# One sum unit per pass in two output projections, and an earlier output bias, in an RG-LRU and latent-attention decoder kernel

## The chip, the cores and the metric

The kernel runs on one core of a Trainium2 chip. The metric is the device time of one launch in microseconds; each kernel's time is the median of its runs.

## What is computed (the reference, cut)

A trunk of two layers over 256 positions of width 2048, all in float32: an RG-LRU block, a SwiGLU feed-forward network, an attention block with a compressed key and value, and a second feed-forward network.

```
h = x
h = h + rglru_block(rmsnorm(h))     # ... (gelu(gate_br) * rec) @ w_out + b_out
h = h + swiglu(rmsnorm(h))          # D_FF = 5632
k, v = shared_kv(rmsnorm(h))
h = h + mla_block(rmsnorm(h), k, v) # ... o.reshape(256, 2048) @ w_o
h = h + swiglu(rmsnorm(h))
```

The change concerns the two square products of 2048 by 2048, `... @ w_out + b_out` and `... @ w_o`. They are called projections here, with d = 0 (LRU) and d = 2 (attention); the down products of the feed-forward networks are d = 1 and d = 3.

## The kernel before

**Splitting.** Each float32 operand is split in a high part (a copy in the type float32r, made by ScalarE) and a low part (the operand minus the high part, made by VectorE). A product of two tiles is three matmuls: high times high, high times low, low times high. The weights come in chunks of 1 MB: SyncE's queue loads chunk c in a slot of `raw`, ScalarE's `split` writes `w_hi`, VectorE's `split` (L1129) writes the low part and raises `w_lo_done`, and TensorE computes one unit per chunk and raises `chunk_used`.

**Units.** In the projections and the feed-forward networks a chunk is 2 tiles of depth (k) by 2 of width (n), and with the 2 tiles of positions a unit is 8 products, 24 matmuls of 128x512 (`plain_unit`). A sum unit (`sum_unit`) computes the same 8 products as 7 by Winograd's scheme, 21 matmuls. For it VectorE makes four sums of 128x128 of the activations (the sides) and three sums of 128x512 of the weights (`sums`), ScalarE and VectorE split them too, and three of the products of all sum units of a pass gather in the second half of the PSUM banks (`shared`), out of which ScalarE (`p1_out`) and VectorE (`shared_add`, `shared_to_h`) read them and add them to h. Before the change only the feed-forward networks have sum units.

**Projections.** `project(d)` is two passes of 8 units, one for each half of the width; unit n has chunk DOWN_C[d] + n. Half 0 gathers in banks 0 to 3, half 1 in banks 4 to 7. ScalarE and VectorE are in the loop `for n in range(12)`, where iteration n splits chunk n + 4. At units 13 and 14 TensorE also transposes the finished first blocks of h, which the next stage wants. `stationary` splits a group of four tiles of the activations.

**Slots.** There are five slots. A chunk of a feed-forward network has its low part in place (`raw_lo` is `raw`), so its slot is free for the next load at `chunk_used`. The chunks of the other stages have their low parts in `w_lo`, so the slot is free at `w_lo_done`, earlier. The LRU stages use four slots, the attention and its projection four others in the order of `MID_SLOTS`.

**Around them.** The stages are, in order: the recurrent half of the LRU's input product (first block from the start, chunks 0 to 15), the gates (4 chunks), the gelu half (16 chunks, called gelu chunks 0 to 15), projection 0, up and down of the network, the attention, projection 2, up and down. The order on every engine is that of the program, written by hand; nothing is reordered. In the gelu stage ScalarE also makes exponentials, squares, tanh and square roots for the scan, and VectorE's `gain_of_input` (L1587, L1590) and the scans stand between the splits. GpSimd adds the output bias to h (L1827): two instructions of 128x2048, after a load of 1 MB of its own, behind a wait on `y_done` 4, the end of the gelu stage. GpSimd also makes half of the low part of two chunks per block of the network (L1850).

Of the kernel before, what the change touches and what calls it, by code (L numbers as in the profile page):

```python
# [18 lines left out]
F32 = mybir.dt.float32  # L19
# [6 lines left out]
P = 128  # L26
# [119 lines left out]
def build_program(nc, a, out):  # L146
    x, positions = a["x"], a["positions"]
    ctx = ExitStack()
    with ctx:
# [24 lines left out]
        raw_lo_t = sb("raw_lo", [P, SLOTS, KC, W], F32R)  # L174
        w_hi_t = sb("w_hi", [P, SLOTS, KC, W], F32R)
# [238 lines left out]
        def _(sp_):  # L414
# [5 lines left out]
            def load(c, src, dst=None):  # L420
# [7 lines left out]
                else:  # L428
                    sp_.wait_ge(chunk_used if in_ffn(before) else w_lo_done, before + 1)
# [225 lines left out]
        def _(act):  # L655
# [74 lines left out]
            def split_sums(c, q, e, tiles=UP_TILES, g_no=None):  # L730
# [19 lines left out]
            def down_split(f, n):  # L750

                c = DOWN_C[2 * f + 1] + n
                if down_sum(n):
                    g_no = down_sum_no(n)
                    split_sums(c, down_unit_no(f, n), g_no % 2, DOWN_TILES, 2 * len(DOWN_SUMS) * f + g_no)
                else:
                    split(c)

            def two_pass(f):
                d = 2 * f + 1  # L760
                c0 = DOWN_C[d]

                def p1_out(n, half):

                    act.wait_ge(chunk_used, c0 + n + 1)
                    act.wait_ge(h_shared, 2 * f + half)
                    A.activation(gtmp[:, 0, :], banks_of(half == 0)[1][0][:, :], ACT.Copy).then_inc(p1_done, 1)

                for n in range(DOWN_UNITS - 4):
# [3 lines left out]
                    if v == DOWN_SUMS[-1]:  # L773
                        p1_out(n, half)
# [27 lines left out]
            def project(d):  # L802
                for n in range(KT - 4):
                    if d == 0 and n == 5:
                        rope_sines()
                    if n in (1, 3) or n == d == 0:
                        g = (n + 3) // 2
# [4 lines left out]
                    split(DOWN_C[d] + n + 4)  # L812
# [309 lines left out]
        def _(dve):  # L1122
# [94 lines left out]

            def down_sums(f, n):

                d, g_no = 2 * f + 1, down_sum_no(n)  # L1220
                v, o, j = n % PASS_UNITS, 2 * len(DOWN_SUMS) * f + g_no, g_no % 3
                dve.wait_ge(gT_act, FB * f + v // 2 + 1)
                slot_free(dve, DOWN_C[d] + n)
                a11, a21 = feat[:, 2 * v, 0:P], feat[:, 2 * v, P:SEQ]
                a12, a22 = feat[:, 2 * v + 1, 0:P], feat[:, 2 * v + 1, P:SEQ]
                V.tensor_tensor(s_raw[:, j, 0, :], a22, a21, ALU.subtract).then_inc(g_sum_step, 1)
                V.tensor_tensor(s_raw[:, j, 2, :], a11, a21, ALU.subtract)
                dve.wait_ge(g_sum_step, 2 * o + 1)
                V.scalar_tensor_tensor(out=s_raw[:, j, 1, :], in0=s_raw[:, j, 0, :], scalar=-1.0, in1=a11,
                                       op0=ALU.mult, op1=ALU.subtract).then_inc(g_sum_step, 1)  # L1230
                dve.wait_ge(g_sum_step, 2 * o + 2)
                V.tensor_tensor(s_raw[:, j, 3, :], a12, s_raw[:, j, 1, :], ALU.add).then_inc(g_sum, 1)
                sums(DOWN_C[d] + n, down_unit_no(f, n), g_no % 2, DOWN_TILES)

            def down_split(f, n):

                c = DOWN_C[2 * f + 1] + n
                if down_sum(n):
                    g_no = down_sum_no(n)
                    o, j = 2 * len(DOWN_SUMS) * f + g_no, g_no % 3  # L1240
                    dve.wait_ge(g_sum_hi, o + 1)
                    V.tensor_tensor(s_lo[:, j, :, :], s_raw[:, j, :, :], s_hi[:, j, :, :].bitcast(F32),
                                    ALU.subtract).then_inc(g_sum_lo, 1)
# [6 lines left out]
            def results_to_h(d, half, units):  # L1250

                result = pass_banks(d, half)
                if d % 2:
                    dve.wait_ge(h_shared, d + half)
                elif d == 0 and half == 0:
                    dve.wait_ge(bout_added, 1)
# [29 lines left out]

            def project(d):
                for n in range(KT - 4):
                    if n in (1, 3) or n == d == 0:
                        g = (n + 3) // 2  # L1290
# [3 lines left out]
                    split(DOWN_C[d] + n + 4)  # L1294
                into_next(d, DOWN_C[d] + KT, KT // 2)

            def two_pass(f):
                d = 2 * f + 1

                def shared_to_h(half):  # L1300

                    n = 4 * f + 2 * half
                    shared_add(banks_of(half == 0)[1], SUM_BLOCKS * f + FB + half,
                               (FB + 2) * f + FB + half)
                    for t in range(NT):
                        hb = h[:, t, (2 * half) * W:(2 * half + 1) * W]
# [1041 lines left out]
```

## Time and profile before

| | |
|---|---|
| median of 3 runs | 1965.88 us (1965.7 to 1966.6) |
| the profiled execution | 1965.88 us, of which its span is 1964.1 us |
| granted TensorE clock, mean | 1.00 of 2.4 GHz |
| TensorE busy | 1956.0 us, 100% |
| VectorE, ScalarE, GpSimd busy | 1728.3, 1168.4, 163.3 us |
| DMA | 378.62 MB, mean 193 GB/s |

Busy times are shares of one execution. A busy TensorE is one whose matmuls overlap without a gap; its speed is read from the starts of two matmuls, not from the duration of one.

### The profile page before, as it was taken

The page shows a single profiled execution, that of the slowest core. Times are in us where ns is not written, and L with a number is a line of the kernel's source. Part 1 is how long each engine was busy: PE and PEld are TensorE (multiplying, and loading weights), DVE is VectorE, ACT ScalarE, POOL GpSimd, SP SyncE. Part 2 cuts the span into 40 slices and gives each one's busy share as a digit, 9 for nine tenths or more (in the row PEclk, how much of TensorE's full clock was granted, in tenths as well). Part 3 has the DMA queues.
Part 4 walks back from the last instruction along what each step waited for, and adds up shares of the span by engine and source line. Part 5 has one row for each costly group of instructions (what it writes and reads, how often), then busy time and mean ns, then how long its engine had stood idle before and what let it go on. Part 6 is the DMA issues. An engine that isn't in the chain of part 4 may idle for free.

```text
span 1964.1 us, 23870 instructions
## 1 busy us (share of the span) xinstructions
PE 1956.0 (100%) x9342; PEld 1645.4 (84%) x9342; DVE 1728.3 (88%) x1957; ACT 1168.4 (59%) x1477; POOL 163.3 (8%) x147
## 2 busy tenths in 40 slices
PE   9999999999999999999999999999999999999999
PEld 8898888888888888888898888888888888888887
DVE  8979847999999999999976886489999999999997
ACT  5488546556565556666666664566555565666563
POOL 1000210110001101000002110000001100010000
PEclk9999999999999999999999999999999999999999
DMA  8654663665666656666564335456565666666664
GB/s 283 209 199 164 222 215 129 196 208 196 200 207 196 208 196 198 209 195 205 180 222 148 115 127 194 143 180 210 196 209 198 200 200 201 205 201 201 205 197 148
DMA packets 160685, 378.62 MB, mean 193 GB/s; under 512 B 6298, under 2 KB 11172, under 8 KB 160452
## 3 DMA queue, kind: packets, MB, share of 16 engines
q1 hardware_dynamic: 160276, 376.06, 58.0%
q8 instruction: 69, 1.13, 0.2%
q0 software_dynamic: 272, 1.13, 0.2%
q14 instruction: 36, 0.29, 0.0%
q10 hardware_dynamic: 32, 0.01, 0.0%
HBM read 375.08 MB, written 2.10 MB: 192 GB/s over the span
## 4 chain that ended last, share of the span: by engine, by line
PE 93%; issue 5%; DVE 1%; POOL 1%; ACT 0%; DMA 0%; POOLq 0%; SPq 0%; ACTq 0%
PE bank L1938 78%; PE bank L2134 6%; PE bank L2132 3%; PE bank L1899 2%; PE bank L1931 1%; PE bank L2118 1%; PE bank L1922 1%; DVE w_lo L1129 0%; POOL stats L1880 0%; PE bank L2131 0%; DMA raw<-in_lru_w_in 0%; ACT w_hi L663 0%; POOL stats L1878 0%; PE bank L2098 0%; POOL stats L1876 0%
## 5 line engine op out<-in xcount | busy, mean ns | idle before, releaser
L1938 PE MATMUL bank<-w_hi,act 128*128 128x512 f32 x3416 | 1097.7, 390 | 0.0
L1938 PEld LDWEIGHTS bank<-w_hi,act 128*128 128x128 f32 x3416 | 641.4, 188 | 132.5
L1938 PE MATMUL bank<-raw_lo,act 128*128 128x512 f32 x1452 | 565.2, 389 | 0.0
L663 ACT ACTIVATE w_hi<-raw 128x2048 fp32r<-128x2048 f32 (+2 forms) x238 | 444.3, 1882 | 143.6 <-PE bank L1938 62.8
L1938 PEld LDWEIGHTS bank<-raw_lo,act 128*128 128x128 f32 x1452 | 272.7, 188 | 56.2
L744 ACT ACTIVATE w_lo<-t_raw 128x1024 fp32r<-128x1024 f32 x110 | 116.4, 1058 | 278.6 <-DVE t_raw L1186 278.6
L1129 DVE TENSOR_TENSOR raw_lo<-raw,w_hi 128x2048 fp32r<-128x2048 f32 x110 | 250.3, 2286 | 9.6 <-ACT w_hi L663 9.4
L1199 DVE TENSOR_TENSOR raw_lo<-raw,w_hi 128x2048 fp32r<-128x2048 f32 x110 | 251.1, 2283 | 0.0
L1129 DVE TENSOR_TENSOR w_lo<-raw,w_hi 128x2048 fp32r<-128x2048 f32 (+1 forms) x84 | 183.1, 2190 | 64.4 <-ACT w_hi L663 64.0
L1938 PE MATMUL bank<-w_lo,act 128*128 128x512 f32 x586 | 192.5, 389 | 0.0
L1850 POOL TENSOR_TENSOR raw_lo<-raw,w_hi 128x1024 fp32r<-128x1024 f32 x44 | 106.7, 2425 | 821.1 <-ACT gtmp L849 738.0
L2134 PE MATMUL bank<-act,w_hi 128*128 128x512 f32 x480 | 169.0, 396 | 0.0
L1938 PE MATMUL bank<-w_lo 128*128 128x512 f32 x528 | 148.2, 389 | 0.0
L2132 PE MATMUL bank<-act,w_lo 128*128 128x256 f32 x512 | 142.6, 281 | 0.2 <-DVE act L1150 0.2
L1186 DVE TENSOR_TENSOR t_raw<-raw 128x1024 f32<-128x1024 f32 x110 | 134.1, 1219 | 0.8 <-issue 0.2
L1195 DVE TENSOR_TENSOR w_lo<-t_raw,w_lo 128x1024 fp32r<-128x1024 f32 x110 | 134.1, 1219 | 0.3 <-ACT w_lo L744 0.3
L1938 PEld LDWEIGHTS bank<-w_lo,act 128*128 128x128 f32 x586 | 110.0, 188 | 22.6
L1899 PE MATMUL bank<-w_hi,act 128*128 128x512 f32 (+2 forms) x448 | 124.5, 354 | 0.3 <-DVE act L1150 0.2
L1938 PE MATMUL bank<-w_hi,w_lo 128*128 128x512 f32 x352 | 122.7, 389 | 0.0
L741 ACT ACTIVATE w_hi<-raw 128x1024 fp32r<-128x1024 f32 x110 | 115.5, 1050 | 3.8 <-DMA raw<-in_ffn_w_in 3.2
L1938 PEld LDWEIGHTS bank<-w_lo 128*128 128x128 f32 x528 | 99.1, 188 | 20.6
L2134 PEld LDWEIGHTS bank<-act,w_hi 128*128 128x128 f32 x480 | 90.1, 188 | 21.2
(246 smaller groups left out, 2403.9 us busy)
## 6 DMA issues: line engine op xcount, KB each, us to landing
raw<-in_ffn_w_in SPq DMA_DIRECT2D x176, 1024.0 KB, 5.4
raw<-in_ffn_w_out SPq DMA_DIRECT2D x88, 1024.0 KB, 5.3
raw<-in_lru_w_in SPq DMA_DIRECT2D x28, 1024.0 KB, 5.6
raw<-in_lru_w_out SPq DMA_DIRECT2D x16, 1024.0 KB, 4.9
raw<-in_w_o SPq DMA_DIRECT2D x16, 1024.0 KB, 5.5
raw<-in_w_ukv SPq DMA_DIRECT2D x8, 1024.0 KB, 5.4
raw<-in_w_uq SPq DMA_DIRECT2D x8, 768.0 KB, 4.6
raw<-in_w_dkv SPq DMA_DIRECT2D x8, 576.0 KB, 3.9
```

Source lines behind the costliest of these rows:

```text
L663: A.activation(flat_chunk(w_hi, SLOT[c], size), flat_chunk(raw, SLOT[c], size), ACT.Copy).then_inc(w_hi_done, 1)
L741: A.activation(hi[:, first, :], own[:, first, :], ACT.Copy)
L744: A.activation(sum_hi_tiles(e)[:, 0:2, :], sum_tiles(t_raw, e)[:, 0:2, :], ACT.Copy).then_inc(sum_hi, 1)
L1129: V.tensor_tensor(low_part(c).rearrange("p k n -> p (k n)")[:, 0:size], flat_chunk(raw, SLOT[c], size), flat_chunk(w_hi, SLOT[c], size).bi ...
L1186: V.tensor_tensor(t13, first, second, ALU.add).then_inc(t_sum, 1)
L1195: V.tensor_tensor(sum_tiles(w_lo_t, e)[:, 0:2, :], sum_tiles(t_raw, e)[:, 0:2, :], sum_hi_tiles(e)[:, 0:2, :].bitcast(F32), ALU.subtract)
L1199: V.tensor_tensor(flat_chunk(raw_lo, SLOT[c], KC * W), flat_chunk(raw, SLOT[c], KC * W), flat_chunk(w_hi, SLOT[c], KC * W).bitcast(F32), A ...
L1850: G.tensor_tensor(raw_lo[SLOT[c]][:, own, :], raw[SLOT[c]][:, own, :], w_hi[SLOT[c]][:, own, :].bitcast(F32), ALU.subtract).then_inc(pool_ ...
L1899: i = T.matmul(outs[t], x_part, wp, start=first and n == 0, stop=last and n == 2)
L1938: i = T.matmul(bank[:, :], x_part, w_part, start=first and n == 0, stop=last and n == 2)
L2132: i = T.matmul(lru_bank(idx, q), wl, act_hi[:, k, :], start=False, stop=False)
L2134: i = T.matmul(bank, wh, x_both, start=False, stop=k == KT - 1)
```

## The change

In each pass of the two projections one unit becomes a sum unit: unit 4 of half 0 and unit 11 of half 1. For that:

- the low parts of both projections' chunks are in place, so their slots are free at `chunk_used`. Projection 2 now has five slots (`slot_of`), projection 0 still four;
- ScalarE and VectorE make the sides and sums of chunks 4 and 11 in iterations 0 and 7, and `shared` is read out in iterations 4 and 11;
- `stationary` of group 2 moves from iteration 1 to 0, that of group 3 from 3 to 2;
- TensorE waits at unit 8, and ahead of the transposes of units 13 and 14, until `shared` has been read;
- the bias is loaded in the high part of slot 4 near the start, and added behind a wait on the last product of the gates (`ix_done` 8) and no more on `y_done` 4. `bout_added` is now awaited by `shared_to_h`.

The other hunks are new counts of the same semaphores, and functions taken out of `two_pass` and `down_sums` word for word.

```diff
+PROJ_SUMS = (4, 11)
...
 def slot_of(c):
-    if not in_ffn(c):
-        return c % 4 if c < C_UP0 else MID_SLOTS[c % 4]
-    return (c - C_UP0) % SLOTS if c < C_DKV else (c - C_UP1 + 2) % SLOTS
+    if c < C_UP0:
+        return c % 4
+    if c < C_DKV:
+        return (c - C_UP0) % SLOTS
+    return MID_SLOTS[c % 4] if c < C_WO else (c - C_WO + 2) % SLOTS
...
-                    sp_.wait_ge(chunk_used if in_ffn(before) else w_lo_done, before + 1)
+                    sp_.wait_ge(chunk_used if in_place(before) else w_lo_done, before + 1)
...
             def project(d):        # ScalarE
                 for n in range(KT - 4):
-                    if n in (1, 3) or n == d == 0:
-                        g = (n + 3) // 2
+                    for g in {0: (2,) if d else (1, 2), 2: (3,)}.get(n, ()):
                         stationary(d, g, wo_slot(g) if d else act_slot(g))
...
-                    split(DOWN_C[d] + n + 4)
+                    if n in PROJ_SHARED:
+                        p1_out(d, PROJ_SHARED[n], n // PROJ_UNITS)
+                    after = n + 4
+                    if after in PROJ_SUMS:
+                        split_sums(DOWN_C[d] + after, proj_unit_no(d, after), PROJ_PLACE[after], DOWN_TILES,
+                                   proj_side_no(d, after), PROJ_SET[after])
+                    else:
+                        split(DOWN_C[d] + after)
...
+            def proj_sums(d, n):        # VectorE
+                kt = 2 * proj_rows(d, n)
+                source_ready(dve, d, kt // 4)
+                dve.wait_ge(chunk_used, DOWN_C[d])
+                make_side(proj_side_no(d, n), kt, PROJ_SET[n])
+                sums(DOWN_C[d] + n, proj_unit_no(d, n), PROJ_PLACE[n], DOWN_TILES)
+            def proj_split(d, n):
+                if n not in PROJ_SUMS:
+                    return split(DOWN_C[d] + n)
+                side_low(proj_side_no(d, n), PROJ_SET[n])
+                split_sums(DOWN_C[d] + n, proj_unit_no(d, n), PROJ_PLACE[n])
...
             def project(d):        # VectorE
                 for n in range(KT - 4):
-                    if n in (1, 3) or n == d == 0:
-                        g = (n + 3) // 2
+                    for g in {0: (2,) if d else (1, 2), 2: (3,)}.get(n, ()):
                         stationary(g, wo_slot(g) if d else act_slot(g), DOWN_G0[d] + g + 1)
                     if n == KT // 2 - 1:
                         results_to_h(d, 0, KT // 2)
-                    split(DOWN_C[d] + n + 4)
+                    if n in PROJ_SHARED:
+                        half = n // PROJ_UNITS
+                        if half:
+                            dve.wait_ge(h_sq, NB * d + 2)
+                        shared_to_h(d, half, SUM_BLOCKS * (d // 2) + half)
+                    if n + 4 in PROJ_SUMS:
+                        proj_sums(d, n + 4)
+                    proj_split(d, n + 4)
...
             rstd(SS_X, RS, 2, D, x_rstd)        # GpSimd
-            pool.wait_ge(y_done, 4)
             pool.dma_start(bout[:, :], a["lru_b_out"][0:1, :].broadcast_to([P, D])).then_inc(bout_in, 16)
             pool.wait_ge(bout_in, 16)
+            pool.wait_ge(ix_done, 8)
             for t in range(NT):
                 i = G.tensor_tensor(h[:, t, :], h[:, t, :], bout[:, :], ALU.add)
...
+                if n == PROJ_UNITS:        # TensorE
+                    pe.wait_ge(u_done, SUM_BLOCKS * (d // 2) + 1)
                 pe.wait_ge(w_lo_done, DOWN_C[d] + n + 1)
-                if v == KT // 2 - 1:
+                if n in PROJ_SUMS:
+                    first = n in (PROJ_SUMS[0], PROJ_SUMS[1])
+                    pe.wait_ge(g_sum_lo, proj_side_no(d, n) + 1)
+                    if first and half:
+                        pe.wait_ge(h_done, NB * d + 2)
+                    elif first and d == 0:
+                        pe.wait_ge(act_hi_done, HI0[0])
+                    elif first:
+                        pe.wait_ge(s_max, 2 * PAIRS)
+                        pe.wait_ge(o_done, PAIRS)
+                    i = sum_unit(c, PROJ_PLACE[n], PROJ_SET[n], k0, result, shared_banks(d, half), first,
+                                 n in PROJ_LAST, None, DOWN_TILES)
+                elif v == KT // 2 - 1:
                     i = last_unit(c, k0, result)
```

## Rows read from the trace of the kernel before

**Rows 1.** The page: busy time of TensorE, its share of the span, instructions.
```profile
PE 1956.0 (100%) x9342; PEld 1645.4 (84%) x9342; DVE 1728.3 (88%) x1957; ACT 1168.4 (59%) x1477; POOL 163.3 (8%) x147
```
**Rows 2.** Busy time by stretch: gelu chunks 11 to 15, projection 0, one network block.
```profile
187.10:214.80 27.70, 27.70 (x161) 24.26 (x161) 25.36 (x35) 13.12 (x14) 0.00 (x0) 1.00 0.76 260
214.80:303.60 88.80, 88.80 (x401) 73.72 (x400) 55.01 (x39) 46.43 (x55) 19.70 (x19) 1.00 0.54 191
343.90:385.70 41.80, 41.80 (x190) 34.61 (x189) 39.60 (x39) 24.74 (x30) 4.83 (x2) 1.00 0.61 201
```
**Rows 3.** Timeline of VectorE, start and length in us: one sum unit's preparation.
```profile
834.52 0.29 DVE L1226 TENSOR_TENSOR t_raw<-feat_all 128x128 f32<-128x128 f32 x1
835.46 1.22 DVE L1186 TENSOR_TENSOR t_raw<-raw 128x1024 f32<-128x1024 f32 x1
842.07 0.69 DVE L1202 TENSOR_TENSOR w_lo<-t_raw,w_lo 128x512 fp32r<-128x512 f32 x1
```
**Rows 4.** Timelines of TensorE, ScalarE and VectorE where projection 2 begins.
```profile
1191.78 0.47 PE L1938 MATMUL bank<-w_hi,act 128*128 128x512 f32 x1
1192.55 1.91 ACT L663 ACTIVATE w_hi<-raw 128x2048 fp32r<-128x2048 f32 x1
1194.36 1.05 ACT L719 ACTIVATE act<-feat_all 128x1024 fp32r<-128x1024 f32 x1
1194.50 2.29 DVE L1129 TENSOR_TENSOR w_lo<-raw,w_hi 128x2048 fp32r<-128x2048 f32 x1 [5.96 <-ACT w_hi L663]
1205.76 1.92 ACT L663 ACTIVATE w_hi<-raw 128x2048 fp32r<-128x2048 f32 x1 [3.52 <-PE bank L1938]
```
**Rows 5.** The tile bout; then GpSimd and VectorE where they are both at work.
```profile
L1827 POOL TENSOR_TENSOR h<-h,bout x2: 6360/6510/6659, 228.3 to 234.7; 128x2048 f32<-128x2048 f32 x2
233.35 3.49 DVE L1129 TENSOR_TENSOR w_lo<-raw,w_hi 128x2048 fp32r<-128x2048 f32 x1 [3.15 <-ACT w_hi L663]
236.76 5.64 DVE L1171 TENSOR_TENSOR act<-feat_all,act 128x1024 fp32r<-128x1024 f32 x1
343.89 2.42 POOL L1850 TENSOR_TENSOR raw_lo<-raw,w_hi 128x1024 fp32r<-128x1024 f32 x1 [35.99 <-ACT gtmp L849]
343.78 0.69 DVE L1210 TENSOR_TENSOR utmp<-gtmp,bank 128x512 f32<-128x512 f32 x1 [2.43 <-ACT gtmp L849]
```
**Rows 6.** Timelines of VectorE, ScalarE and TensorE from the gates to gelu chunk 11.
```profile
126.69 0.69 DVE L1579 TENSOR_TENSOR feat_all<-feat_all,utmp 128x512 f32<-128x512 f32 x1 [0.56 <-ACT utmp L938]
128.49 2.29 DVE L1129 TENSOR_TENSOR w_lo<-raw,w_hi 128x2048 fp32r<-128x2048 f32 x1 [1.11 <-ACT w_hi L663]
138.46 1.23 DVE L1587 SCALAR_TENSOR_TENSOR feat_all<-feat_all 128x1024 f32<-128x1024 f32 x1 [3.42 <-ACT feat_all L960]
141.86 1.06 ACT L958 ACTIVATE feat_all<-feat_all 128x1024 f32<-128x1024 f32 x1
184.61 2.27 DVE L1129 TENSOR_TENSOR w_lo<-raw,w_hi 128x2048 fp32r<-128x2048 f32 x1
187.05 0.28 PE L2132 MATMUL bank<-act,w_lo 128*128 128x256 f32 x1
```
**Rows 7.** The start: one stretch of 10 us, VectorE's split of chunk 7, ScalarE behind chunk 7's unit.
```profile
20.00:30.00 10.00, 10.00 (x62) 8.75 (x60) 8.81 (x16) 7.46 (x13) 1.81 (x2) 1.00 1.05 341
46.11 2.29 DVE L1129 TENSOR_TENSOR w_lo<-raw,w_hi 128x2048 fp32r<-128x2048 f32 x1
56.15 1.21 ACT L923 ACTIVATE utmp<-bank 128x256 f32<-128x256 f32 x4 [3.57 <-PE bank L2134]
```
**Rows 8.** DMA issues (count, size, median us to landing); ScalarE and VectorE at projection 0's end.
```profile
raw<-in_ffn_w_in SPq DMA_DIRECT2D x176, 1024.0 KB, 5.4
raw<-in_lru_w_out SPq DMA_DIRECT2D x16, 1024.0 KB, 4.9
295.68 0.84 ACT L687 ACTIVATE act<-bank,cols 128x256 fp32r<-128x256 f32 x2 [1.63 <-PE bank L1922]
298.81 0.88 DVE L1150 SCALAR_TENSOR_TENSOR act<-bank,cols,act 128x256 fp32r<-128x256 f32 x2 [0.58 <-ACT feat_all L692]
```

More of the change, by code:

```diff
@@ L174, in build_program @@
         raw_lo_t = sb("raw_lo", [P, SLOTS, KC, W], F32R)
+        with ExitStack() as over:
+            sb("w_hi_0_3", [P, SLOTS - 1, KC, W], F32, over)
+            bout = sb("bout", [P, D], F32, over)
         w_hi_t = sb("w_hi", [P, SLOTS, KC, W], F32R)
@@ L643, in pass_banks, with shared_banks @@
             return banks if d % 2 else [banks[n] for n in (0, 2, 1, 3)]
+        def shared_banks(d, half):
+            return banks_of((half + d) % 2 == 1)[1]
         def sum_tiles(t, e):
@@ L773, in two_pass @@
                     if v == DOWN_SUMS[-1]:
-                        p1_out(n, half)
+                        p1_out(d, n, half)
                     if n % 2:
@@ L1216, in shared_add, with make_side @@
                 dve.wait_ge(u_done, n_done + 1)
+            def make_side(o, kt, j):
+                a11, a21 = feat[:, kt, 0:P], feat[:, kt, P:SEQ]
+                a12, a22 = feat[:, kt + 1, 0:P], feat[:, kt + 1, P:SEQ]
+                to = s_raw[:, j, :, :]
+                V.tensor_tensor(to[:, 0, :], a22, a21, ALU.subtract).then_inc(g_sum_step, 1)
+                V.tensor_tensor(to[:, 2, :], a11, a21, ALU.subtract)
+                dve.wait_ge(g_sum_step, 2 * o + 1)
+                V.scalar_tensor_tensor(out=to[:, 1, :], in0=to[:, 0, :], scalar=-1.0, in1=a11,
+                                       op0=ALU.mult, op1=ALU.subtract).then_inc(g_sum_step, 1)
+                dve.wait_ge(g_sum_step, 2 * o + 2)
+                V.tensor_tensor(to[:, 3, :], a12, to[:, 1, :], ALU.add).then_inc(g_sum, 1)
@@ L1225, in down_sums @@
[L1225 to L1230, printed above, removed]
@@ L1252, in results_to_h @@
                 result = pass_banks(d, half)
[L1253 to L1256, printed above, removed]
+                dve.wait_ge(h_shared, 2 * d + half + 1)
                 for b in (0, 1):
@@ L1285, in into_next, with shared_to_h @@
                     split(c_next + n)
+            def shared_to_h(d, half, n_shared):
+                if d == half == 0:
+                    dve.wait_ge(bout_added, 1)
+                shared_add(shared_banks(d, half), n_shared, n_shared)
+                for t in range(NT):
+                    hb = h[:, t, (2 * half) * W:(2 * half + 1) * W]
+                    V.tensor_tensor(hb, hb, gtmp[:, t, :], ALU.add)
+                for t in range(NT):
+                    hb = h[:, t, (2 * half + 1) * W:(2 * half + 2) * W]
+                    i = V.tensor_tensor(hb, hb, mix[:, t, :], ALU.subtract)
+                i.then_inc(h_shared, 1)
             def project(d):
                 for n in range(KT - 4):
-                    if n in (1, 3) or n == d == 0:
-                        g = (n + 3) // 2
+                    for g in {0: (2,) if d else (1, 2), 2: (3,)}.get(n, ()):
                         stationary(g, wo_slot(g) if d else act_slot(g), DOWN_G0[d] + g + 1)
@@ L1298, in two_pass @@
                 d = 2 * f + 1
[L1300 to L1306, printed above, removed]
-                        V.tensor_tensor(hb, hb, gtmp[:, t, :], ALU.add)
-                    for t in range(NT):
-                        hb = h[:, t, (2 * half + 1) * W:(2 * half + 2) * W]
-                        i = V.tensor_tensor(hb, hb, mix[:, t, :], ALU.subtract)
-                    i.then_inc(h_shared, 1)
                 for n in range(DOWN_UNITS - 4):
@@ L1976, in sum_unit @@
                 product(shared[3], s3, t3, first, last)
-                if first:
+                if first and gT_needed:
                     pe.wait_ge(gT_act, gT_needed)
```

78 lines of the change are left out of this document (45 added, 33 removed).

## The prediction, made before the changed kernel was run

> **What bounds the kernel now.** I read the page first: TensorE is busy for 1956.0 of 1964.1 us [rows 1], so only two things can move the time, fewer matmuls and new waits of TensorE. Then busy time by stretch, to get the pace [rows 2]: projection 0 has 16 x 24 = 384 matmuls of 128x512 and 16 transposes in 88.80 us. ScalarE's splits follow the units that free their slots, 1.92 of work and 3.52 of waiting, so a plain unit is 5.44 us [rows 4] (these rows are of the other projection); 5.44 / 24 = 0.2267 us for a matmul, 87.05 us for the 384, which leaves 1.75 us for the transposes (0.87 for the eight at unit 13, and again at unit 14). A network block of 4 plain and 4 sum units has 180 matmuls and 8 transposes: 180 x 0.2267 + 0.87 = 41.7, against 41.80 in its row, so a sum unit runs at the same pace. Last the timelines of ScalarE, VectorE and GpSimd at each place that the change touches, to find what time each wait has to spare. In these stretches the granted clock is 1.00 of 2.4 GHz.
>
> **What is removed.** Three matmuls in each of four units: 12 x 0.2267 = **2.72 us**. This is certain and it is all that the change can remove from TensorE. Moving the bias frees VectorE in projection 0 (beside GpSimd a split, 2.29 elsewhere, took 3.49, and a `stationary` of 128x1024, a size that takes 1.22 elsewhere, 5.64 [rows 3 to 5]), but TensorE had no wait there, so that gives nothing.
>
> **What is added, projection 2, unit 4.** A sum unit's preparation on VectorE takes from 834.52 to 842.76, 8.24 us, from the first side to the last low part [rows 3]: 0.94 of sides, then 7.3. Before, VectorE sits idle for 5.96 us until 1194.50, then makes chunk 4's low part in 2.29 [rows 4]. The idle time doesn't help: in program order `stationary` of group 2 now comes first, and it waits for ScalarE, which is held until 1192.55 by the attention's last copy. So: ScalarE 1192.55 + 1.05, VectorE's `stationary` 1193.64 to 1194.77 (1.22 for its size [rows 3], the last 0.09 beside the next instruction), sides and sums and splits + 8.24 = 1203.0. TensorE wants unit 4 after half of unit 2 and unit 3, 36 matmuls from 1191.78 [rows 4], at 1199.95. All its waits stand ahead of the unit, none of it can start early: **+3.1 us**. Bounds: 0 if something lets VectorE begin in its idle time (I see nothing that does), 3.4 if signals cost more. Behind it the five slots leave time: unit 5's split ends 2.2 us later and isn't wanted for 4.76.
>
> **Projection 0, unit 4.** Here the load comes at the release of unit 0, 214.80 + 5.44 + 0.2, lands 4.9 later [rows 8] at 225.4, and 7.3 us of VectorE end at 232.7; wanted at 214.80 + 4 x 5.44 = 236.6. Hidden, 3.9 to spare.
>
> **Unit 11.** VectorE ends the split of chunk 10 at 261.5 (release of unit 6 at 252.2, + 0.2 + 4.9 + 1.9 + 2.3), adds half 0 to h (2.5), then 8.24: 272.3, wanted at 214.80 + 11 x 5.44 - 0.68 = 274.0. Hidden, 1.7 to spare. In projection 2 chunks come a unit earlier, 6 to spare.
>
> **Reading out `shared`.** Four adds of 0.69 [rows 5] after the split of the chunk before. Half 0 has 14 us. For half 1 in projection 0: unit 10 ends at 274.0, chunk 14 lands at 279.1, ScalarE to 281.0, VectorE to 283.3, adds to 286.1; the transposes want it at 214.80 + 13 x 5.44 - 1.36 + 2.72 = 286.9. Hidden by 0.8.
>
> **The loads of the next stage.** With four slots in place, the network's chunk 1 is loaded only when unit 13 ends, at 214.80 + 14 x 5.44 - 1.36 + 0.87 = 290.5. It lands at + 0.2 + 5.4 [rows 8] = 296.1, ScalarE splits it until 298.0, and only then, in program order, makes the tiles of block 1. From ScalarE's start on them to VectorE's end took 295.68 to 299.69, 4.0 us: 302.0. TensorE wants them at 303.6 - 1.36 = 302.2. Too close to call: I take **+0.2**, bounds 0 and 1.5 (a landing of 7 us).
>
> **The bias at the gates.** The two instructions of GpSimd took 6.36 and 6.66 us [rows 5]. The rows read as turns: VectorE's split at 233.35 ends 2.15 after the first of them does (234.69), its 128x1024 instruction at 236.76 ends 1.09 after the second (241.31). So one engine waits for the other's whole instruction, GpSimd's own work being some 4.5 us each. An add from PSUM at 343.78 wasn't held (0.69 beside GpSimd's 2.42) [rows 5]. The Trainium skill says so too (GPSIMD Engine Reference, the table of its opening): GpSimd's SBUF interfaces are shared with VectorE, in contention with instructions that have two SBUF inputs. By that rule and by the rows alike, the bias costs VectorE time wherever it goes; the rule speaks against the new place, but gives no other sum.
>
> At the gates: the last product ends at 127.4 [rows 6], GpSimd runs 127.6 to 132.1, the split that began at 128.49 ends at 134.3, GpSimd's second to 138.8, the next split to 141.0 (2.2 each), and L1587 and L1590, which ended at 140.4, end at 142.9. ScalarE's L958, at 141.86, waits for them: 1.0 late. From there to gelu chunk 11 ScalarE and VectorE hand work to each other with no idle time that absorbs it, and chunk 11's low part was ready at 186.88 for a unit that began at 187.05 [rows 6]. 1.0 less 0.2 to spare: **+0.8 us**. Bounds: 0 if GpSimd's turns fall in VectorE's gaps (1.11 and 3.42 us), 2.8 if L1587 is held as long as the instruction of 5.64 was (4.4 us over its own time, less the 1.4 that L958 had).
>
> **The bias load at the start.** Another 1 MB where the DMA engines are full (share 1.05, 341 GB/s [rows 7]) is 3.1 us for chunks 5 and 6. VectorE had some 0.9 us between chunk 6 and its split, so it is 2.2 late, and its convolution stands between that and chunk 7. Chunk 7's low part was ready at 48.4; the unit after it ends before 56.15 and a unit is 27.7 / 5 = 5.54 us [rows 2, 7], so it is wanted at 50.4, 2.0 later. **+0.2 us**, bounds 0 and 1.1.
>
> **Sum.** -2.72 + 3.1 + 0.2 + 0.8 + 0.2 = +1.6 us. The profiled execution took 1965.88 us (span 1964.1 and 1.8 around it), which is also the median of the runs: **1967.5 us**.
>
> **Rivals.** 0.2% is 3.9 us, about what a measurement of this kernel can tell from no change.
>
> *All new waits are hidden.* VectorE begins unit 4's sums earlier than I see, or GpSimd's turns do no harm: 1965.88 - 2.72 = 1963.2, or up to 1965.5 with one of the two. For it: 5.96 us of idle VectorE ahead of the place. Against: the program order. 18 in 100.
>
> *The clock falls (the other side).* TensorE's idle time is 8.1 us in the whole span [rows 1]; a wait of 3.1 us in one piece would be new, and the rows know no level but 1.00. If the clock went to its lower level, 1.2 GHz, a matmul would take 2 x 0.2267, and the 21 of the unit 4.76 us more: 1972.2. It decides from 2.3 us on, ten matmuls at the lower level. The Trainium skill (TensorE: Matmul & The Clock Gate, Part 1) says that the clock is halved after TensorE has been idle and comes back only with sustained work; no run here shows it yet. 7 in 100.
>
> *GpSimd's turns cost the upper bound*, with landings late as well: + 2.0 on the gates, + 1 at the network's start: 1970.5. 5 in 100.
>
> *Faster.* All else hidden gives 1963.2; another 1.3 us would be needed, a pace quicker by 0.7% over the 177 us of both projections, and no row shows a pace that depends on where the low parts lie. 4 in 100.
>
> **From this.** Forecast, unit 4 of projection 2 waits some 3 us and the total is between 1965.5 and 1969.5: 66 in 100. With the hidden case that is 84 within 0.2%; 12 slower, 4 faster. The range from 1963.2, the floor of the hidden case, to 1970.0 leaves out half of the slow cases and the fast one.
>
> **What would show it.** TensorE's waits: one of about 3 us ahead of unit 4 of projection 2, on VectorE; none at unit 4 or 11 of projection 0 nor unit 11 of projection 2; one of 0.8 at gelu chunk 11 and perhaps small ones at chunk 7 and the network's first unit. Twelve matmuls fewer. GpSimd's two instructions from 127.6, and L1587's end near 142.2. L1129 and L1171 in projection 0 back at 2.29 and 1.22. I am wrong if unit 4 of projection 2 doesn't wait, if the clock leaves 1.00, or if the wait at the gates is over 2 us.

## The result, and the profile after

| | before | after |
|---|---|---|
| median | 1966.29 us (1965.67 to 1967.59, 17 runs) | 1969.87 us (1967.73 to 1971.72, 17 runs) |
| span of the profiled execution | 1964.1 us | 1968.4 us |
| TensorE busy, matmuls | 1956.0 us, 9342 | 1955.8 us, 9330 |

The ratio is 1.0017, with an interval from 1.001 to 1.0024: slower by some 3.4 us, inside the 0.2% that I called no change. The forecast was 1967.5 us, 2.4 under the median; of these 0.4 are the kernel before, whose median of 17 runs is 1966.29 where the forecast started from 1965.88.

The page's busy times, and the longest of TensorE's waits (in total, times, longest), against [rows 1]:

```profile
PE 1955.8 (99%) x9330; PEld 1643.8 (84%) x9330; DVE 1772.7 (90%) x2029; ACT 1179.5 (60%) x1501; POOL 163.5 (8%) x147
...
PE bank L2000 <- issue: 2.9, 1, 2.9
PE bank L2180 <- POOL ident L1861: 1.5, 1, 1.5
PE bank L2209 <- DVE w_lo L1165: 1.2, 1, 1.2
```

The matmuls are 12 fewer, but TensorE's busy time is only 0.2 us less, where 12 x 0.2267 would be 2.7. So beside two new waits (2.9 and 1.2 us; the 1.5, near the start, stands in the kernel before too) some matmuls became slower. The granted clock tells which. These are VectorE and TensorE at the start of projection 2 after the change (start, duration, idle time before), then busy time by stretch with the clock in the third column from the right, against [rows 4]:

```profile
1194.05 1.23 DVE L1207 TENSOR_TENSOR act<-feat_all,act 128x1024 fp32r<-128x1024 f32 x1 [5.09 <-ACT act L749]
1195.19 0.28 DVE L1259 TENSOR_TENSOR t_raw<-feat_all 128x128 f32<-128x128 f32 x1
...
1202.73 0.68 DVE L1238 TENSOR_TENSOR w_lo<-t_raw,w_lo 128x512 fp32r<-128x512 f32 x1
...
1200.25 0.39 PE L2000 MATMUL bank<-w_hi,act 128*128 128x512 f32 x1
1203.51 0.47 PE L2000 MATMUL bank<-w_hi,act 128*128 128x512 f32 x1 [2.87 <-issue]
...
1202.00:1204.00 2.00, 0.49 (x2) 0.48 (x3) 2.00 (x3) 2.00 (x3) 0.00 (x0) 0.97 0.84 281
1204.00:1206.00 2.00, 2.00 (x6) 1.52 (x6) 2.00 (x2) 2.00 (x2) 0.00 (x0) 0.50 0.56 223
1206.00:1208.00 2.00, 2.00 (x8) 1.58 (x7) 2.00 (x2) 0.74 (x1) 0.00 (x0) 0.67 0.00 0
1208.00:1210.00 2.00, 2.00 (x11) 1.62 (x9) 2.00 (x2) 0.00 (x0) 0.00 (x0) 1.00 0.00 0
```

VectorE sits idle for 5.09 us, makes the stationary tiles, then the sums, and ends at 1203.41. TensorE started its last matmul at 1200.25 and the next at 1203.51, 3.26 us later instead of 0.23: a wait of 3.0 us. From 1204 the clock is at 0.50, its lower level of 1.2 GHz, and that stretch of 2 us counts 6 matmuls where those at 1.00 count 10 or 11; at 1208 it is back.

The other place is the gates: GpSimd, VectorE and ScalarE there, and TensorE at gelu chunk 11, against [rows 6]:

```profile
127.78 11.31 POOL L1889 TENSOR_TENSOR h<-h,bout 128x2048 f32<-128x2048 f32 x2 [102.36 <-DVE feat_all L1641]
...
128.72 12.51 DVE L1165 TENSOR_TENSOR w_lo<-raw,w_hi 128x2048 fp32r<-128x2048 f32 x2 [1.11 <-ACT w_hi L693]
141.16 1.21 DVE L1649 SCALAR_TENSOR_TENSOR feat_all<-feat_all 128x1024 f32<-128x1024 f32 x1
...
143.19 1.06 ACT L994 ACTIVATE feat_all<-feat_all 128x1024 f32<-128x1024 f32 x1 [1.21 <-DVE feat_all L1652]
...
185.93 2.27 DVE L1165 TENSOR_TENSOR w_lo<-raw,w_hi 128x2048 fp32r<-128x2048 f32 x1
...
188.25 0.39 PE L2209 MATMUL bank<-act,w_lo 128*128 128x256 f32 x1 [1.21 <-DVE w_lo L1165]
```

Two of VectorE's splits, 4.5 us of work, stand there with 12.51 us; the row of ScalarE that was to be 1.0 late starts at 143.19, 1.33 later than before; and TensorE waits at gelu chunk 11.

Matching the two traces matmul by matmul gives how much later the same matmul starts than in the kernel before. Each removed unit's worth (0.68 us) shows as a step down:

| at (us of before) | later by | between this row and the one above |
|---|---|---|
| 30 | +0.24 | +0.18 already at 20 us |
| 150 | -0.17 | |
| 187.05 | +1.31 | the wait at gelu chunk 11 |
| 214.8 | +1.82 | no wait in between |
| 300 | +0.44 | units 4 and 11 of projection 0 |
| 1190 | +0.42 | |
| 1260 | +3.86 | wait and clock at unit 4, units 4 and 11 of projection 2 |
| the last | +4.32 | no wait in between |

At 1260 the step is 3.44 = 3.03 of wait - 1.36 for the two units' removed matmuls + 1.77. Of the 1.77 the lower clock is **1.6 us**: seven matmuls start 0.43 us after the one before instead of 0.227, and one on either side 0.36 and 0.30. The rest is the restart (0.1, which stands behind such a wait at a clock of 1.00 too, see e6) and a few hundredths of pace.

### The profile page after: what moved, and what is told of

Same layout as the page of the kernel before. It is cut to its first block, busy times and chain, and to the rows that moved or that the text cites. A ratio compares the mean times of both kernels' runs of the same rounds, so it can differ in the third digit from the quotient of the medians.

```text
span 1968.4 us, 23973 instructions
## 1 busy us (share of the span) xinstructions
PE 1955.8 (99%) x9330; PEld 1643.8 (84%) x9330; DVE 1772.7 (90%) x2029; ACT 1179.5 (60%) x1501; POOL 163.5 (8%) x147
## 4 chain that ended last, share of the span: by engine, by line
PE 89%; issue 5%; DVE 3%; ACT 1%; POOL 1%; DMA 0%; POOLq 0%; SPq 0%; ACTq 0%
PE bank L2000 78%; PE bank L2211 4%; PE bank L1961 2%; PE bank L2209 2%; DVE w_lo L1165 1%; PE bank L1993 1%; PE bank L2195 1%; PE bank L1984 1%; ACT w_hi L693 0%; DVE feat_all L1662 0%; POOL stats L1942 0%; DMA raw<-in_lru_w_in 0%; DVE feat_all L1659 0%; DVE raw_lo L1165 0%; PE bank L2208 0%
## 5 line engine op out<-in xcount | busy, mean ns | idle before, releaser
L2000 PE MATMUL bank<-w_hi,act 128*128 128x512 f32 x3368 | 1085.3, 390 | 2.9 <-issue 2.9
L2000 PEld LDWEIGHTS bank<-w_hi,act 128*128 128x128 f32 x3368 | 632.4, 188 | 134.0 <-issue 3.3
L2000 PE MATMUL bank<-raw_lo,act 128*128 128x512 f32 x1684 | 655.7, 389 | 0.0
L693 ACT ACTIVATE w_hi<-raw 128x2048 fp32r<-128x2048 f32 (+2 forms) x234 | 436.9, 1881 | 126.4 <-DMA raw<-in_ffn_w_in 34.2
L2000 PEld LDWEIGHTS bank<-raw_lo,act 128*128 128x128 f32 x1684 | 316.3, 188 | 65.2
L1165 DVE TENSOR_TENSOR raw_lo<-raw,w_hi 128x2048 fp32r<-128x2048 f32 x138 | 314.0, 2286 | 28.6 <-ACT w_hi L693 28.2
L1235 DVE TENSOR_TENSOR raw_lo<-raw,w_hi 128x2048 fp32r<-128x2048 f32 x114 | 260.2, 2283 | 0.0
L2000 PE MATMUL bank<-w_lo 128*128 128x512 f32 x552 | 155.0, 389 | 0.0
L1165 DVE TENSOR_TENSOR w_lo<-raw,w_hi 128x2048 fp32r<-128x2048 f32 (+2 forms) x52 | 116.5, 2255 | 11.4 <-ACT w_hi L693 11.2
L2209 PEld LDWEIGHTS bank<-act,w_lo 128*128 128x128 f32 x512 | 96.6, 189 | 2.7 <-DVE w_lo L1165 1.5
L768 ACT ACTIVATE w_lo<-t_raw 128x512 fp32r<-128x512 f32 x32 | 20.3, 633 | 128.0 <-DVE t_raw L1265 128.0
```

The costliest lines, as they stand in the source:

```text
L693: A.activation(flat_chunk(w_hi, SLOT[c], size), flat_chunk(raw, SLOT[c], size), ACT.Copy).then_inc(w_hi_done, 1)
L1165: V.tensor_tensor(low_part(c).rearrange("p k n -> p (k n)")[:, 0:size], flat_chunk(raw, SLOT[c], size), flat_chunk(w_hi, SLOT[c], size).bi ...
L1235: V.tensor_tensor(flat_chunk(raw_lo, SLOT[c], KC * W), flat_chunk(raw, SLOT[c], KC * W), flat_chunk(w_hi, SLOT[c], KC * W).bitcast(F32), A ...
L2000: i = T.matmul(bank[:, :], x_part, w_part, start=first and n == 0, stop=last and n == 2)
L2209: i = T.matmul(lru_bank(idx, q), wl, act_hi[:, k, :], start=False, stop=False)
```

## The experiments

**e1: only the bias moved.** The kernel before, with the bias loaded at the start and added behind the gates.

```diff
+        with ExitStack() as over:
+            sb("w_hi_0_3", [P, SLOTS - 1, KC, W], F32, over)
+            bout = sb("bout", [P, D], F32, over)
...
-            pool.wait_ge(y_done, 4)
             pool.dma_start(bout[:, :], ...)
             pool.wait_ge(bout_in, 16)
+            pool.wait_ge(ix_done, 8)
```

> The kernel before with the bias loaded and added as in the change, and nothing else. My theory: GpSimd's two instructions hold VectorE's at the gates, ScalarE's square starts some 1.3 us late, and TensorE waits some 1.4 us at gelu chunk 11; that is nearly all the bias costs, 1.0 to 1.9 us in the span with the pace of the stretches around it, and projection 2 keeps its time. Rival, the load at the start costs: TensorE is late by 1 us or more at 60 us already. Rival, harmless: span within 0.3 us of the kernel before.

Measured: 1967.87 us (1966.95 to 1968.65, 10 runs) against 1966.65, ratio 1.0006 [0.9996, 1.0015]. The interval includes 1, but the trace has the place. TensorE's wait at gelu chunk 11 and GpSimd's two instructions:

```profile
PE bank L2135 <- DVE w_lo L1132: 1.2, 1, 1.2
...
127.94 11.31 POOL L1830 TENSOR_TENSOR h<-h,bout 128x2048 f32<-128x2048 f32 x2 [102.36 <-DVE feat_all L1582]
```

From 150 to 187.05 us TensorE falls behind by 1.48, and by 0.50 more up to 214.8: the same two figures as in the changed kernel. So the wait at chunk 11 and the 0.5 behind it belong to the bias, not to the sum units.

**e8: only the early load.** As e1, but the add stays behind `y_done` 4.

```diff
-            pool.wait_ge(ix_done, 8)
+            pool.wait_ge(y_done, 4)
```

> The kernel before with the bias only loaded at the start, and added behind y_done 4 as before. If the early load costs nothing, the time is that of the kernel before within 0.5 us (1966 to 1967.2), there is no new wait of TensorE, and gelu chunk 11 doesn't wait. If the 1 MB at the start delays a chunk, TensorE is later by 0.2 to 1.1 us behind chunk 7, at 50 us, beyond the few tenths by which runs differ at 20 us already, and the time is higher by as much.

Measured: 1966.04 us (one run), before 1966.11. Lateness +0.35 at 20 us, before the load is issued, +0.35 at 56 and at 124.9, and between 150 and 187.05 +0.29 without any wait at chunk 11. The load costs nothing. The 0.29 has nothing to do with the bias and goes off the 1.48 of e1: the wait is worth **1.2 us**, as its own row says.

**e2 and e3: only a late chunk.** The kernel before, with three (e2) or two (e3) extra VectorE instructions of 128x2048 ahead of chunk 4's low part in projection 2; they write that low part early.

```diff
+                    if d == 2 and n == 0:
+                        c = DOWN_C[d] + 4
+                        dve.wait_ge(w_hi_done, c + 1)
+                        for _ in range(3):
+                            step(V.tensor_tensor(low_part(c)..., raw, w_hi, ALU.subtract))
                     split(DOWN_C[d] + n + 4)
```

> The kernel before with three more instructions of 128x2048 on VectorE ahead of the low part of chunk 4 of projection 2, which makes that chunk late but has no sum unit. Theory, the clock follows the wait: TensorE waits 3.3 to 3.6 us at unit 4, the granted clock is 0.50 for some 3 us after it, and the span grows by 5.0 to 5.3 us. Rival, the fall of the clock comes from the sum unit: the wait as long, the clock 1.00, the span + 3.4 us.

> The same with two more instructions. Theory: TensorE waits 1.0 to 1.4 us at unit 4, the granted clock stays 1.00, the span + 1.0 to 1.4 us. Rival, any wait lowers the clock: + 2.7 us or more.

Measured: e2 1972.99 us, e3 1968.65 us (one run each), before 1966.65. TensorE in e2 at unit 4, then the clock:

```profile
1205.06 0.80 PE L1944 MATMUL bank<-w_hi,act 128*128 128x512 f32 x1 [4.73 <-DVE act L1171]
...
1206.00:1208.00 2.00, 2.00 (x6) 1.53 (x5) 2.00 (x2) 0.00 (x0) 0.00 (x0) 0.50 0.98 375
```

In e2 TensorE waited 4.73 us, longer than I had aimed at, since the extra work also holds group 2's tiles. There is no sum unit in this kernel and the clock falls all the same, so the fall comes with the wait. In e3 TensorE waited 2.41 us, for 1.0 to 1.4 aimed at, and the clock didn't fall: 2.7 us later behind it, 0.3 more than the wait. e2 was 7.0 later, so its lower clock cost some 7.0 - 4.73 - 0.3 = 2.0. I took the difference for a dependence on the length, and **e12** ran e3's kernel again, timed:

> The kernel of e3 (before, with two more VectorE instructions of 128x2048 ahead of chunk 4's low part in projection 2, thus a wait of 2.4 us and no other edit), timed, to see in how many runs its clock falls. If a wait of 2.4 us can bring the fall, as in e7, the runs lie in two groups: some 1968.7 us at a mean clock of 1.000, and 1 to 3 us above it at 0.999 or less. If e3 shows the rule for this length, all runs are within 1968.0 to 1969.5 us at 1.000, and the falls of e6 and e7 need another reason than the length of the wait.

Measured: 1969.56 us (1968.86 to 1971.6, 10 runs), ratio 1.0014 [1.0005, 1.0024]. Six runs lie at 1968.86 to 1969.62 with a mean clock of 1.000, four at 1970.91 to 1971.6 with 0.999. The traces of e3 and of e12 are of one kernel; the matmul behind the wait in each, then the clock by stretch:

```profile
1202.19 0.50 PE L1944 MATMUL bank<-w_hi,act 128*128 128x512 f32 x1 [2.41 <-DVE act L1171]
...
1202.00:1204.00 2.00, 1.81 (x8) 1.51 (x9) 2.00 (x2) 0.00 (x0) 0.00 (x0) 1.00 0.75 211
1204.00:1206.00 2.00, 2.00 (x11) 1.65 (x10) 2.00 (x2) 0.00 (x0) 0.00 (x0) 1.00 1.02 356
```

```profile
1202.80 0.50 PE L1944 MATMUL bank<-w_hi,act 128*128 128x512 f32 x1 [2.41 <-DVE act L1171]
...
1202.00:1204.00 2.00, 1.20 (x4) 1.02 (x5) 2.00 (x2) 0.40 (x1) 0.00 (x0) 0.85 0.64 133
1204.00:1206.00 2.00, 2.00 (x6) 1.54 (x6) 2.00 (x2) 0.00 (x0) 0.00 (x0) 0.50 0.93 365
```

The same wait, the same work on both sides of it, and the clock falls in one execution and not in the other. The fall costs 1.9 us by the medians of the two groups (1971.01 and 1969.11), and 1.6 by the two traces (4.3 us later behind the wait, and 2.7). My reading of e3 alone was wrong.

**e4: unit 5 for unit 4.** The changed kernel with `PROJ_SUMS = (5, 11)`, and the four tables beside it to match.

> The changed kernel with unit 5 instead of unit 4 as the sum unit of half 0 in both projections. Theory, unit 4 is late because VectorE starts only when the attention is over: with a unit more of lead TensorE waits 0 to 0.5 us at unit 5 of projection 2, the clock stays 1.00, and the span falls by 4.3 to 4.8 us against the changed kernel, to some 1964. Rival, the lateness moves along with the unit: the wait is 2 us or more at unit 5.

Measured: 1965.64 us (1965.12 to 1966.49, 10 runs) against 1966.65, ratio 0.9994 [0.9985, 1.0004]; 4.2 under the changed kernel. The clock is 1.00 in all stretches, and projection 2 has a wait of 0.27 us left:

```profile
PE bank L2209 <- DVE w_lo L1165: 1.2, 1, 1.2
...
PE bank L2000 <- DVE w_lo L1238: 0.3, 1, 0.3
```

**e5 and e11: another order.** The changed kernel with unit 4; in projection 2 VectorE makes the sides and sums of chunk 4 ahead of group 2's tiles.

```diff
             def project(d):        # VectorE
                 for n in range(KT - 4):
+                    if d == 2 and n == 0:
+                        proj_sums(d, 4)
...
-                    if n + 4 in PROJ_SUMS:
+                    if n + 4 in PROJ_SUMS and (d == 0 or n):
                         proj_sums(d, n + 4)
```

> The changed kernel with one move: in projection 2 VectorE makes the sides and the weight sums of chunk 4 ahead of the stationary tiles of group 2, in the 5 us in which it sat idle; nothing else is changed. If the order on VectorE is what makes unit 4 late, the wait ahead of it falls from 3.05 to some 0.7 us (ScalarE's copies of the sums still come behind the attention's last copy), the granted clock stays at 1.00 around 1206, and the run takes 1969.9 - 2.35 - 1.7 = about 1965.9 us. If ScalarE alone sets the end of the chain, the wait stays near 3 us, the clock falls again and the time stays at 1969 to 1970.

> The kernel of e5 again, timed, for an interval. If order and clock explain the whole of unit 4's cost, the median is at 1965.3 to 1966.0 us, and every run has a mean clock of 1.000. If the one run of e5 was a lucky one, some runs are at 1967 to 1969 us with a clock of 0.999, as those of the changed kernel are.

Measured: e5 1965.55 us (one run); e11 1965.83 us (1965.02 to 1966.51, 10 runs), ratio 0.9995 [0.9986, 1.0005], every run at a mean clock of 1.000. VectorE and TensorE in e5:

```profile
1191.64 0.69 DVE L1226 TENSOR_TENSOR t_raw<-raw 128x512 f32<-128x512 f32 x1
1193.91 1.22 DVE L1207 TENSOR_TENSOR act<-feat_all,act 128x1024 fp32r<-128x1024 f32 x1 [1.58 <-ACT act L749]
...
1200.19 0.69 DVE L1238 TENSOR_TENSOR w_lo<-t_raw,w_lo 128x512 fp32r<-128x512 f32 x1
...
1200.97 0.47 PE L2002 MATMUL bank<-w_hi,act 128*128 128x512 f32 x1 [0.48 <-issue]
```

The sums are made in the time in which VectorE waited for ScalarE, the low parts end at 1200.88 instead of 1203.41, and the next matmul starts 0.86 us after the last, a wait of 0.63. The order of two steps on one engine was worth 4.0 us, by the medians (1969.87 and 1965.83) and by the lateness that projection 2 adds in the two traces, of which 2.4 is the wait and the rest the clock.

**e6: the bias in pieces, late in the gelu stage.** The changed kernel, but eight GpSimd instructions of 128x512 behind `y_done` 3.

```diff
-            pool.wait_ge(ix_done, 8)
+            pool.wait_ge(y_done, 3)
             for t in range(NT):
-                i = G.tensor_tensor(h[:, t, :], h[:, t, :], bout[:, :], ALU.add)
+                for b in range(NB):
+                    hb = h[:, t, b * W:(b + 1) * W]
+                    i = G.tensor_tensor(hb, hb, bout[:, b * W:(b + 1) * W], ALU.add)
```

> The changed kernel with the bias added in eight GpSimd instructions of 128x512, behind y_done 3 (late in the gelu stage), in place of two of 128x2048 behind the gates. If GpSimd's turns are what delays gelu chunk 11, its wait of 1.2 us is gone and no other comes in its place: a turn is a quarter as long, some 1.1 us; time 1969.9 - 1.3 = about 1968.6 us. If the delay moves on, a wait of about 1 us stands at a later gelu chunk or at unit 4 of projection 0 and the time stays at 1969.9. Unit 4 of projection 2 waits 3 us as before, with the clock at its lower level for a few us behind it.

Measured: 1971.49 us (1970.39 to 1973.8, 6 runs), ratio 1.0029 [1.0017, 1.0041]: a miss. The wait at chunk 11 is gone, but unit 2 of projection 0 waits 2.44 us for the `stationary` of group 1. GpSimd, VectorE and TensorE:

```profile
204.33 12.94 POOL L1891 TENSOR_TENSOR h<-h,bout 128x512 f32<-128x512 f32 x8 [178.01 <-DVE feat_all L1697]
...
208.53 1.28 DVE L1481 TENSOR_SCALAR ang<-ang 128x64 f32<-128x64 f32 x1
209.85 1.22 DVE L1482 TENSOR_SCALAR ang<-ang 128x64 f32<-128x64 f32 x1
...
217.35 0.20 DVE L1489 TENSOR_SCALAR ang<-ang 128x64 f32<-128x64 f32 x1
227.99 2.35 DVE L1207 TENSOR_TENSOR act<-feat_all,act 128x1024 fp32r<-128x1024 f32 x2
...
229.26 0.79 PE L2002 MATMUL bank<-w_hi,act 128*128 128x512 f32 x1 [2.44 <-DVE act L1207]
```

A VectorE instruction of 128x64 takes 0.20 us when GpSimd has ended, and 1.2 while it works: each of VectorE's short instructions waits for one piece of GpSimd's. Seven in a row lost about 1 us each, and the split ahead of them as much. So shorter pieces made each turn shorter and gave more of them: eight of 1.0 us here, against two of 4.4 with whole instructions. Whether two whole instructions at this place would have done less harm wasn't run; e6 changes the place and the size together.

The clock fell behind this first wait (the stretches stand under e7). Unit 4 of projection 2 waits as long as in the changed kernel's trace, and there the clock stays at 1.00:

```profile
1206.75 0.47 PE L2002 MATMUL bank<-w_hi,act 128*128 128x512 f32 x1 [2.88 <-issue]
...
1207.00:1209.00 2.00, 2.00 (x10) 1.62 (x10) 2.00 (x2) 2.00 (x2) 0.00 (x0) 1.00 0.73 283
```

By the same matching as above, with the three removed matmuls added back, TensorE loses 3.14 us at unit 4 here and 4.76 in the changed kernel: 1.6 for the clock once more.

**e7: e4 and e6 together.**

> The changed kernel with unit 5 for unit 4 and with the bias in eight pieces behind y_done 3. If the two costs are apart and add, this is 1965.6 - 1.3 = about 1964.4 us, below both kernels, some 2 us (0.1%) under the kernel before: the 2.72 us of the twelve matmuls less about 0.6 of small waits. If there is a third cost that the others hid, it stays at 1965.6.

Measured: 1967.78 us (1966.14 to 1969.72, 11 runs), ratio 1.0009 [1.0, 1.0018]: a miss for the same reason, with the same wait of 2.44 us in projection 0. Seven runs have a mean clock of 0.999 (1967.14 to 1969.72 us), four 1.000 (1966.14 to 1966.95). Behind that wait the clock fell in e6's trace and not in e7's; the two stretches of each:

```profile
228.00:230.00 2.00, 0.74 (x2) 0.65 (x3) 2.00 (x3) 0.37 (x1) 0.00 (x0) 0.72 0.80 289
230.00:232.00 2.00, 2.00 (x7) 1.51 (x6) 1.97 (x6) 0.63 (x2) 0.00 (x0) 0.50 0.54 221
```

```profile
228.00:230.00 2.00, 1.45 (x6) 1.23 (x7) 2.00 (x3) 1.47 (x1) 0.00 (x0) 1.00 0.97 391
230.00:232.00 2.00, 2.00 (x10) 1.62 (x10) 2.00 (x3) 0.00 (x0) 0.00 (x0) 1.00 0.26 100
```

**e9: the order of e5, and the bias where VectorE has pauses.** The two instructions of 128x2048 come behind the low parts of chunk 4 of projection 0. **e10** does the same with unit 5.

```diff
-            pool.wait_ge(ix_done, 8)
+            pool.wait_ge(w_lo_done, DOWN_C[0] + 5)      # e10: + 6
```

> The changed kernel with the order of e5 (VectorE's sides and sums of chunk 4 ahead of group 2 in projection 2) and with the bias added once the sum unit of projection 0 has its low parts (behind the w_lo_done of its chunk 4), some 234 us, where VectorE has pauses of 1.9 and 3.1 us between whole splits and no short instructions to be held one by one. If the two instructions of GpSimd find these pauses, no unit of projection 0 waits, gelu chunk 11 doesn't wait (1.2 us less), and the time is that of e5 less 1.2, some 1964.4 us, with the granted clock at 1.00 in every run. If the turns only move the harm, a unit of projection 0 behind unit 5, or the reading out of the shared banks, is late, with a wait of 1 to 3 us, and the time is 1965.5 us or more.

> The changed kernel with unit 5 for unit 4, as e4, and the bias behind the low parts of chunk 5 of projection 0, some 239 us. Expected: e4's 1965.6 less the 1.2 us wait at gelu chunk 11, some 1964.4 us, with only the 0.3 us wait at unit 5 of projection 2 left of the change. Rival: GpSimd's two instructions of 4.5 us each, that now begin at 239 and alternate with two splits and the stationary tiles, end later than the reading out of the shared banks wants them (252 us) and hold a split: a wait of 1 us or more in projection 0, 1965.6 us or more.

Measured: e9 **1964.83 us** (1964.13 to 1965.84, 11 runs) against 1966.61, ratio 0.999 [0.9981, 0.9999]; it beats both kernels, 1.8 us under the kernel before, with an interval that just leaves out 1. e10: 1965.72 us (1964.6 to 1966.58, 11 runs), ratio 0.9994 [0.9985, 1.0003], no better than e4. VectorE and TensorE in e9, then VectorE in e10, while GpSimd adds the bias (232.89 to 244.12 and 238.56 to 250.64):

```profile
232.96 6.69 DVE L1165 TENSOR_TENSOR raw_lo<-raw,w_hi 128x2048 fp32r<-128x2048 f32 x1 [0.23 <-ACT w_hi L693]
239.57 5.63 DVE L1207 TENSOR_TENSOR act<-feat_all,act 128x1024 fp32r<-128x1024 f32 x1
...
247.55 0.47 PE L2002 MATMUL bank<-w_hi,act 128*128 128x512 f32 x1 [0.46 <-DVE raw_lo L1165]
```

```profile
239.45 15.60 DVE L1165 TENSOR_TENSOR raw_lo<-raw,w_hi 128x2048 fp32r<-128x2048 f32 x3
254.97 0.68 DVE L1246 TENSOR_TENSOR utmp<-gtmp,bank 128x512 f32<-128x512 f32 x1
```

In e9 two instructions are held for 4.4 us each, and the pauses behind them absorb most of it; unit 6 waits 0.5 us, after which TensorE is 0.7 later. So both readings on record hold in part: no wait at chunk 11 any more, a smaller one in its place, 1.7 - 0.7 = 1.0 us in all, which is also the difference of the medians of e11 and e9. In e10 two of three splits in a row are held (15.60 us for 6.9 of work), the reading out of `shared` begins at 254.97 instead of 252.42 in e4, and TensorE waits in two places, the splits behind at 252.8 and unit 11 at 275.3, 1.25 us later in all. Its rival held in the time and in the sum, but as two small waits and not one of 1 us.

## Why the prediction was right or wrong

| term | forecast | measured |
|---|---|---|
| 12 matmuls | -2.72 | -2.7, a step of 0.68 at each unit |
| wait at unit 4 of projection 2 | +3.1 | +3.03 |
| the clock behind it | 0 (rival: +4.76) | +1.6 in the trace; below 1.000 in 15 of 17 runs |
| the bias at the gates | +0.8 | +1.2 of wait, and +0.5 behind it |
| the bias load at the start | +0.2 | 0 (e8) |
| the network's first unit | +0.2 | 0, no wait |

**The step that failed** is the price of the wait at unit 4: I priced it at its length alone and gave the fall of the clock 7 in 100. It falls in most executions: 15 of the 17 runs have a mean clock of 0.998 or 0.999 and lie at 1969.15 to 1971.72 us; the two at 1.000 are at 1967.73 and 1968.28, beside the 1967.5 of the forecast. The median of 1969.87 lies inside the range of 1963.2 to 1970.0, but 0.13 under its upper end, and that is luck: the fall of the clock, at the price that I gave it (1972.2), lay outside the range, and by the forecast's own sign ("if the clock leaves 1.00") it was wrong. The rival named the right mechanism with the wrong price. It let all 21 matmuls of the unit run at the lower level, and at twice 0.2267 us; in the trace seven did in full, started from 1204.60 to 1207.16, each 0.43 us after the one before, 0.2 more and not 0.227, and one on either side in part. The rule of the Trainium skill that the rival cited (TensorE: Matmul & The Clock Gate, Part 1) is borne out: the halved clock stands in the stretches behind the wait, and returned with TensorE at work. What I didn't say is that the same wait brings the fall in some executions only. By the runs here: never where the new waits behind the first loads stayed at 1.2 us or less (e1, e4, e5, e9, e10, e11: 53 runs at 1.000), in 4 of 11 and 7 of 11 with one of 2.4 us (e3 with e12, and e7), in 15 of 17 with one of 2.9 us, in 6 of 6 with one of each (e6, where the trace shows it behind the first and not behind the second). One of the 76 runs of the kernel before that were timed beside the experiments has a mean clock of 0.999 too (1968.5 us), so a fall can come without a new wait. What decides it in one execution stays open.

**Unit 4 of projection 2**: right step by step. The stationary tiles started at 1194.05 (forecast 1193.64), the low parts were ready at 1203.41 (1203.0), the wait was 3.03 us (3.1). That the order of the program and not the amount of work made it is shown by e5.

**The gates**: the mechanism was right, the size too small. The forecast had ScalarE's instruction at 142.9; it started at 143.19. The wait is 1.2 us (e1; 0.7 in the trace of e11; absent in e6 to e10, that have no add there). The 0.5 us behind the wait was in none of my terms. It isn't a wait but a slower pace, below. Together they are 1.7 us, for 0.8 forecast.

**Projection 0**: right. The forecast of no wait at units 4 and 11, at the transposes and at the readings of `shared` holds, and `L1129` and `L1171` (L1165 and L1207 after the change) are back at 2.29 and 1.22 us there; that freed nothing on TensorE, as expected:

```profile
234.69 2.29 DVE L1165 TENSOR_TENSOR raw_lo<-raw,w_hi 128x2048 fp32r<-128x2048 f32 x1 [0.34 <-ACT w_hi L693]
236.90 1.22 DVE L1207 TENSOR_TENSOR act<-feat_all,act 128x1024 fp32r<-128x1024 f32 x1
```

**The start and the network's first unit**: both +0.2 were too much. The lateness at 30 us (+0.24) is there at 20 us (+0.18), before the bias load is issued at 24.8; over the other traces it lies between -0.31 and +1.04 at 20 us, from the first loads of x and the weights.

**The sum**: the profiled executions differ by 1968.4 - 1964.1 = 4.3 us in span. From the table of lateness: 0.24 (start) - 0.41 (pace up to 150) + 1.48 + 0.51 (gates) - 2.72 + 4.80 (wait and clock) + 0.44 (the pace of the second network and a remainder of 0.02) = 4.34. The two terms of pace nearly cancel. Against the forecast's +1.6 the clock (1.6) and the gates (0.9) were too low and the two terms of 0.2 too high, so the errors partly cancel as well. One side figure of the forecast doesn't come out of its terms: of the two larger waits hidden one at a time, unit 4's gives 1964.4 and the gates' 1966.7, and not "up to 1965.5"; nothing else rests on it.

## What to carry to other kernels

When TensorE bounds a kernel and gets a new wait of the length seen here (2.4 us or more; 1.2 didn't bring it), price the clock behind it as well, here 1.6 to 2.0 us and in some executions only: a spread of the runs into two groups, with a mean clock of 0.999 in the upper one, is its sign. Before adding work to a busy engine, look at what stands in front of it in program order: making the sums ahead of a step that waits anyway recovered 4.0 us. Work that another engine does isn't free where the two hold each other by whole instructions; put it where the held engine has pauses. Cutting it in pieces isn't a remedy by itself: in e6 it only gave more and shorter turns.

## What the runs showed of the hardware

**Two paces at one clock.** In the LRU's input product, pairs of a matmul of 128x512 and one of 128x256 follow each other at 0.347 or at 0.353 us, with the granted clock at 1.00 in both. Each of the two blocks below has the first and the last start of 16 pairs, in the kernel before and in the one after:

```profile
192.60 0.40 PE L2131 MATMUL bank<-act,w_hi 128*128 128x512 f32 x1
...
198.16 0.27 PE L2132 MATMUL bank<-act,w_lo 128*128 128x256 f32 x1
```

```profile
194.01 0.39 PE L2208 MATMUL bank<-act,w_hi 128*128 128x512 f32 x1
...
199.66 0.28 PE L2209 MATMUL bank<-act,w_lo 128*128 128x256 f32 x1
```

5.56 / 16 = 0.3475 us and 5.65 / 16 = 0.3531 us. In the kernel before the quick pace holds from 187 us; in each of the five traces with a wait at gelu chunk 11 (after, e1, e4, e5, e11) the slow one does, and TensorE loses 0.5 us up to 214.8; in the eight others, without that wait, it loses none. In other stretches the pace changes between traces without any wait (the kernel before is slow from 125 us on, the changed one quick until 147). What sets it stays open; a few tenths of a microsecond by which two traces differ, with no wait, can be this.

**Turns by whole instructions.** GpSimd and VectorE held each other in each of the four new places of the bias (the gates, e6, e9, e10), where GpSimd's 1 MB of sums took 11.2 to 12.9 us; a split of 2.29 us took up to 6.7, one of 128x1024 5.63, a 128x64 instruction 1.2 instead of 0.20. Each was held for about one instruction of GpSimd: 4.4 us beside 128x2048, 1.0 beside 128x512. Four of the seven held instructions of 128x64 (TENSOR_SCALAR) have one input tensor and constants, so here it took no second input to be held.
